# Rows of picks and of weights in the gating stage, built by one comparison and one product for each octet of tokens

## The chip, the cores and the metric

The kernel runs on one core of one Trainium2 chip. The metric is the device time of the core in microseconds (us); lower is better. The engines are TensorE (PE, with its weight loads as PEld), VectorE (DVE), ScalarE (ACT), GpSimd (POOL) and SyncE (SP), which issues most transfers.

## The reference, cut to what matters

Two layers over 256 latent and 256 context tokens of width 1024 are computed: a pooling mixer, then a gated DeltaNet mixer, each followed by a PEER expert mixer. The PEER mixer runs three times (context and latents in layer 0, latents in layer 1):

```python
sc, pos = lax.top_k(cand, PEER_TOPK)
...
eidx = jnp.take_along_axis(cidx, pos, axis=-1)   # 8 heads x 16 experts of 16384 for each token
gate = jax.nn.softmax(sc, axis=-1)
...
act = jax.nn.gelu(jnp.einsum('td,ted->te', xt, jnp.take(u_tab, et, axis=0)), approximate=False)
return jnp.einsum('te,ted->td', gt * act, jnp.take(v_tab, et, axis=0))
```

An expert is a pair (i1, i2) of keys, each of 0 to 127. So the weights of one token are a 128 x 128 matrix with up to 128 entries: the sum over its 128 picks of (one-hot row of i2) times (one-hot row of i1 scaled by the weight).

## The kernel before, in words

The kernel does not gather experts. It computes all 128 blocks of 128 experts for all tokens, multiplies the activations by the weight matrices, and multiplies the result with all of `v_tab`. Each of the three PEER passes (`peer(g, ...)`, g = 0, 1, 2) has these stages:

- **Query and U blocks.** Blocks of 512 KB are loaded to `raw[0..3]`; ScalarE rounds one to `hi` (line 542), VectorE takes the rest `lo` (line 1030), TensorE multiplies (lines 1732 to 1734), ScalarE applies Gelu into `buf` (line 577). VectorE finds the top picks beside it. Late in this stage `pick_pairs` turns the picks and the weights (split into three bf16 parts that sum to the fp32 weight) into bf16 arrays in which each value stands twice (`i1p`, `i2p`, `g_pairs`, by token), and computes the first rows of octets 0 and 1.
- **Gating stage.** 256 tokens are taken as 32 octets of 8 (`OCTET`, `N_OCT`). Even octets use the PSUM pair pG, odd ones pS; row buffers alternate in the same way. For octet o:
  - `first_row` (line 1152, VectorE): one comparison of 8 x 128 bf16 elements, column number against i1. It counts up `first_ready`.
  - `gate_hots` (VectorE): the same comparison against i2 (line 1158), then, after a wait on `first_ready`, three products (line 1162), one for each weight part, of 5 tokens x 128.
  - `gate_rows` or `gate_rows_at` (ScalarE, lines 592 and 600): the rows of the other 3 tokens (`ACT_GATED = 3`), 9 copies of 128 columns with the weight as scale, after a wait on `first_ready`.
  - `gate_octet` or `gate_matmuls` (TensorE, lines 1800 and 1787): 24 bf16 matmuls of 128 columns into one PSUM pair, after waits for VectorE's rows (`onehot`), ScalarE's rows (`rows_gated`) and the release of the PSUM pair by octet o - 2 (`gated`).
  - `apply_gates` (line 1174, VectorE): `buf` times PSUM, 1024 fp32 elements, after a wait on `gates_mm`.
- **V blocks.** As the U blocks, with TensorE lines 1863 to 1867.

VectorE's order in the gating stage is written out: the loop holds, for two octets, `apply_gates(o)`, then `onehot_rows(o + 2)`, which is `first_row` and `gate_hots`. In passes 0 and 1 TensorE also multiplies, behind the matmuls of each of the octets 0 to 27, one 512 KB chunk of the adaLN weights (`mod_chunk`, line 1813; the transfer is SP's line 487), and behind each odd octet from 5 on it turns a row into columns (`mod_columns`, line 1823), after ScalarE copied the row (`mod_row`, line 610). Pass 2 has neither.

At the end of the U blocks VectorE and ScalarE alternate between splitting the first V blocks and the rows of octets 0 and 1, since those rows lie in `raw`, where the last U blocks and the first V blocks were:

```python
for j in range(RING):
    split_lo(None, ku + NE - RING, j + AHEAD)
    if j == 1:
        ve.wait_ge(lo_ready, RING + k0 + NQ + NE)
        gate_hots(None, 0)
ve.wait_ge(lo_ready, RING + k0 + NQ + NE + AHEAD)
gate_hots(None, 1)
```

In loops an instruction whose address depends on the loop counter has a register instruction ahead of it ("ISA" or "REGISTER_ALU" in the order below, FUSED_REGOPS in the trace); where the instruction waits, the wait is on that register instruction.

Of the kernel before, what the change touches and what calls it, by code (L numbers as in the profile page):

```python
# [32 lines left out]
ALU = mybir.AluOpType  # L33
# [48 lines left out]
def build(nc, a, out):  # L82
    ctx = ExitStack()
    with ctx:
# [22 lines left out]
        table = sb("table", [P, 10])  # L107
        gated1 = sb("gated1", [P, 16, P])
        iota_b = sb("iota_b", [P, P], BF16)
# [212 lines left out]

        raw_flat = raw_all[:, :, :, :].rearrange("p r c e -> p (r c e)")
        hots = [halves(raw_flat[:, 2 * D:4 * D], 4, OCTET, P), halves(raw_flat[:, 0:2 * D], 4, OCTET, P)]
        gated_flat = gated1[:, :, :].rearrange("p a b -> p (a b)")
        first_rows = halves(gated_flat[:, 0:D], 2, OCTET, P)
        pairs = halves(gated_flat[:, D:2 * D], 4, T, 2)
        i1p, i2p = pairs[:, 0], pairs[:, 1]
        g_pairs = [pairs[:, 2], pairs[:, 3], halves(gT[:, :], T, 2)]
        bank_pair = [pG_pair, pS_pair]  # L330
# [177 lines left out]
        def _(act):  # L508
# [39 lines left out]
            def peer(g, k0, e0, last):  # L548
# [37 lines left out]
                def gate_rows(n, o):  # L586

                    act.wait_ge(first_ready, 2 * n + (N_OCT * g + o + 1) if n is not None else N_OCT * g + o + 1)
                    for t in range(OCTET - ACT_GATED, OCTET):
                        tok = 16 * n + (8 * o + t) if n is not None else 8 * o + t  # L590
                        for q in range(3):
                            i = s.activation(hots[o % 2][:, 1 + q, t, :], first_rows[:, o % 2, t, :], ACT.Copy, scale=picks[q][:, bass.ds(tok, 1)])  # L592
                    i.then_inc(rows_gated, 1)

                def gate_rows_at(n, o):

                    act.wait_ge(first_ready, OCTET * n + (N_OCT * g + o + 1))
                    for t in range(OCTET - ACT_GATED, OCTET):
                        for q in range(3):
                            i = s.activation(hots[o % 2][:, 1 + q, t, :], first_rows[:, o % 2, t, :], ACT.Copy,  # L600
                                             scale=picks[q][:, bass.ds(OCTET * OCTET * n + (OCTET * o + t), 1)])
                    i.then_inc(rows_gated, 1)
# [286 lines left out]
        def _(ve):  # L889
# [189 lines left out]
            def peer(g, k0, e0, last):  # L1079
# [32 lines left out]
                while b % RING:  # L1112
                    split_lo(None, ku + b, AHEAD)
                    b += 1
                assert b <= 88, b
                def pick_pairs(part):

                    if part == 0:
                        ve.wait_ge(picksT, g + 1)
                        v.tensor_copy(g_pairs[0], twice(pG[1][:, 0:T]))  # L1120
                        link(v.tensor_copy(i1p, twice(pG[0][:, 0:T])))
                    elif part == 1:
                        v.tensor_tensor(g_left, pG[1][:, 0:T], g_pairs[0][:, :, 0], ALU.subtract)
                        link(v.tensor_copy(i2p, twice(pG[0][:, T:2 * T])))
                    elif part == 2:
                        v.tensor_copy(g_pairs[1], twice(g_left))
                        link(v.tensor_copy(picks[0], g_pairs[0][:, :, 0]))
                    elif part == 3:
                        link(v.tensor_tensor(picks[2], g_left, g_pairs[1][:, :, 0], ALU.subtract))
                    elif part == 4:  # L1130
                        v.tensor_copy(g_pairs[2], twice(picks[2]))
                        link(v.tensor_copy(picks[1], g_pairs[1][:, :, 0]))
# [5 lines left out]
                twice = lambda x: x.unsqueeze(2).to_broadcast([P, T, 2])  # L1138

                def spread(x, m):  # L1140
                    return x.rearrange("p t (a b) -> p t a b", b=2)[:, 0:m]

                def per_token(x, tok, m):
                    return x[:, bass.ds(tok, m), :].unsqueeze(2).to_broadcast([P, m, P // 2, 2])

                def octet_cols():
                    return iota_b[:, :].rearrange("p (a b) -> p a b", b=2).unsqueeze(1).to_broadcast([P, OCTET, P // 2, 2])

                def first_row(n, o):

                    tok = 16 * n + 8 * o if n is not None else 8 * o
                    v.tensor_tensor(spread(first_rows[:, o % 2], OCTET), octet_cols(), per_token(i1p, tok, OCTET), ALU.is_equal).then_inc(first_ready, 1)  # L1152

                def gate_hots(n, o):

                    tok = 16 * n + 8 * o if n is not None else 8 * o
                    one, two = first_rows[:, o % 2], hots[o % 2]
                    v.tensor_tensor(spread(two[:, 0], OCTET), octet_cols(), per_token(i2p, tok, OCTET), ALU.is_equal)
                    ve.wait_ge(first_ready, 2 * n + (N_OCT * g + o + 1) if n is not None else N_OCT * g + o + 1)
                    m = OCTET - ACT_GATED  # L1160
                    for q in range(3):
                        i = v.tensor_tensor(spread(two[:, 1 + q], m), spread(one, m), per_token(g_pairs[q], tok, m), ALU.mult)  # L1162
                    i.then_inc(onehot, 1)

                def onehot_rows(n, o):

                    first_row(n, o)
                    gate_hots(n, o)

# [466 lines left out]
        def _(pe):  # L1636
# [111 lines left out]
            def peer(g, k0, e0, last):  # L1748
# [29 lines left out]
                def gate_matmuls(n, o):  # L1778
# [6 lines left out]
                    for t in range(OCTET):  # L1785
                        for q in range(3):
                            mm = t_.matmul(bank_pair[o % 2][:, t // QUAD, (t % QUAD) * P:(t % QUAD + 1) * P], hots[o % 2][:, 0, t, :],
                                           hots[o % 2][:, 1 + q, t, :], start=(q == 0), stop=(q == 2), skip_group_check=True)
                    mm.then_inc(gates_mm, 1)

                def gate_octet(n, o):
# [6 lines left out]
                    for t in range(OCTET):  # L1798
                        for q in range(3):
                            mm = t_.matmul(bank_pair[o % 2][:, t // QUAD, (t % QUAD) * P:(t % QUAD + 1) * P], hots[o % 2][:, 0, t, :],  # L1800
                                           hots[o % 2][:, 1 + q, t, :], start=(q == 0), stop=(q == 2), skip_group_check=True)
                    mm.then_inc(gates_mm, 1)
# [422 lines left out]
```

## Time and profile before

| | |
|---|---|
| median of 3 runs | 3440.96 us (3434.68 to 3442.36) |
| profiled execution | 3437.17 us, its span 3435.4 us |
| TensorE / VectorE / ScalarE busy | 94% / 65% / 48% of the span |
| mean granted TensorE clock | 0.964 of full speed |
| gating stages (first row product to last `apply_gates`) | 544 to 665 us, 1452 to 1573 us, 2944 to 3069 us |

A busy time is the sum of an engine's instruction durations, without overlap. In the timelines below, a start in us is followed by a duration in us; an instruction with no wait in front of it starts before the one ahead of it has ended, so its share of the engine's time is the distance from start to start, and not its duration. Brackets at the end of a line give the idle time before it and what ended that.

### The profile page before, as it was taken

Reading aid. Unit: us, or ns where it says so; the run is one execution under the profiler, and the core shown is the slowest. Engines: PE = TensorE matmul, PEld = TensorE weight load, DVE = VectorE, ACT = ScalarE, POOL = GpSimd, SP = SyncE. Lnnn points to the kernel's source line nnn. Section 1 sums busy time; section 2 is a strip of 40 time slices with the busy share of each in tenths; the row PEclk is TensorE's granted clock in tenths of the full one; section 3 lists DMA queues with packets and bytes.
Section 4 is the critical chain, followed back from the end, with each engine's and each line's share of the span. In section 5 each row is a group of like instructions: output and inputs, shape, how many; then the busy total and the mean of one; then the engine's idle time right before and its main releaser. Section 6 shows DMA issues by size and latency. Waiting matters only on the chain.

```text
span 3435.4 us, 73133 instructions
## 1 busy us (share of the span) xinstructions
PE 3239.5 (94%) x25548; PEld 2864.7 (83%) x25548; DVE 2223.0 (65%) x4624; ACT 1665.2 (48%) x2924; POOL 152.6 (4%) x90
## 2 busy tenths in 40 slices
PE   8999999999999999999999998889889999669998
PEld 4899996588889999957888898877789999658887
DVE  6588957855556887596555673443348884785555
ACT  5544446645444444575545553222234444664544
POOL 0000000000000000000000362011100000000000
PEclk9999999999999999999999998998899999879999
DMA  8555454355565555454656441000145545116664
GB/s 320 172 166 182 165 188 161 129 195 191 196 208 165 182 182 172 161 166 151 216 193 206 151 146 57 3 2 2 44 153 177 183 165 183 48 68 194 204 193 135
DMA packets 143454, 530.33 MB, mean 154 GB/s; under 512 B 16544, under 2 KB 16688, under 8 KB 141040
## 3 DMA queue, kind: packets, MB, share of 16 engines
q1 hardware_dynamic: 141120, 514.01, 45.2%
q0 software_dynamic: 2224, 14.76, 1.2%
q8 instruction: 80, 1.31, 0.2%
q14 instruction: 30, 0.25, 0.0%
HBM read 522.42 MB, written 6.29 MB: 154 GB/s over the span
## 4 chain that ended last, share of the span: by engine, by line
PE 76%; DVE 12%; issue 7%; POOL 2%; ACT 1%; DVEq 1%; DMA 1%; SPq 0%; ACTq 0%; POOLq 0%
PE pS L1732 11%; PE pS L1734 11%; PE pS L1733 11%; PE pY L1863 10%; PE pY L1865 10%; PE pY L1867 10%; PE pY L1925 4%; PE pS L1925 3%; DVE buf L1174 2%; POOL lo L1608 2%; PE pG L1925 2%; DVE raw L1162 2%; DVE gated L1152 1%; DVE lo L1030 1%; DVE buf L1264 1%
## 5 line engine op out<-in xcount | busy, mean ns | idle before, releaser
L1030 DVE TENSOR_TENSOR lo<-raw,hi 128x1024 fp32r<-128x1024 f32 x824 | 1009.4, 1225 | 774.7 <-ACT hi L542 771.5
L542 ACT CAST hi<-raw 128x1024 fp32r<-128x1024 f32 x872 | 913.3, 1048 | 526.3 <-PE pY L1867 510.0
L1732 PE MATMUL pS<-h_hi,hi 128*128 128x256 f32 x3552 | 1013.0, 285 | 32.9 <-DVE lo L1030 9.9
L1733 PE MATMUL pS<-h_lo,hi 128*128 128x256 f32 x3552 | 1007.6, 284 | 0.0
L1734 PE MATMUL pS<-h_hi,lo 128*128 128x256 f32 x3552 | 1007.3, 284 | 0.0
L1732 PEld LDWEIGHTS pS<-h_hi,hi 128*128 128x128 f32 x3552 | 684.2, 193 | 40.3 <-issue 27.6
L1733 PEld LDWEIGHTS pS<-h_lo,hi 128*128 128x128 f32 x3552 | 684.5, 193 | 0.2
L1734 PEld LDWEIGHTS pS<-h_hi,lo 128*128 128x128 f32 x3552 | 684.3, 193 | 0.0
L1863 PE MATMUL pY<-hi,h_hi 128*128 128x512 f32 x1536 | 475.4, 391 | 7.0 <-DVE h_lo L1215 7.0
L1867 PE MATMUL pY<-hi,h_lo 128*128 128x512 f32 x1536 | 474.7, 390 | 0.0
L1865 PE MATMUL pY<-lo,h_hi 128*128 128x512 f32 x1536 | 474.7, 390 | 0.0
L577 ACT ACTIVATE buf<-pS 128x256 f32 x372 | 142.8, 384 | 602.9 <-PE pS L1734 602.9
L1863 PEld LDWEIGHTS pY<-hi,h_hi 128*128 128x128 f32 x1536 | 289.6, 189 | 67.6 <-issue 6.6
L1865 PEld LDWEIGHTS pY<-lo,h_hi 128*128 128x128 f32 x1536 | 289.6, 189 | 60.3
L1867 PEld LDWEIGHTS pY<-hi,h_lo 128*128 128x128 f32 x1536 | 289.5, 188 | 60.4
L592 ACT ACTIVATE raw<-gated,g 128x128 bf16<-128x128 bf16 x576 | 175.2, 388 | 52.9 <-DVE gated L1152 51.9
L1215 DVE TENSOR_TENSOR h_lo<-buf,h_hi 128x256 fp32r<-128x256 f32 x384 | 160.6, 418 | 2.4 <-ACT h_hi L648 2.4
L648 ACT CAST h_hi<-buf 128x256 fp32r x384 | 154.6, 403 | 11.8 <-DVE buf L1174 11.8
L1608 POOL TENSOR_TENSOR lo<-raw,hi 128x1024 fp32r<-128x1024 f32 x48 | 116.1, 2431 | 186.8 <-ACT hi L542 186.6
L1925 PE MATMUL pY<-buf 64*64 64x64 f32 (+2 forms) x2956 | 107.2, 228 | 13.6 <-DVE buf L1451 9.9
L1925 PEld LDWEIGHTS pY<-buf 64*64 64x64 f32 (+2 forms) x2956 | 100.4, 144 | 19.5 <-DVE buf L1451 10.5
L1732 PE MATMUL pY<-h_hi,hi 128*128 128x256 f32 x352 | 103.2, 293 | 8.6 <-POOL lo L1608 5.0
(298 smaller groups left out, 3261.3 us busy)
## 6 DMA issues: line engine op xcount, KB each, us to landing
raw<-in_blocks SPq DMA_DIRECT2D x872, 512.0 KB, 3.3
gate_mod<-in_mod_wT SPq DMA_DIRECT2D x56, 512.0 KB, 3.6
raw<-in_mod_wT SPq DMA_DIRECT2D x20, 512.0 KB, 9.4
buf<-in_mod_wT SPq DMA_DIRECT2D x20, 512.0 KB, 8.2
buf<-in_keysT POOLq DMA_DIRECT2D x3, 1024.0 KB, 5.5
buf<-in_window SPq DMA_DIRECT2D x2, 1024.0 KB, 11.7
spill_x_res<-buf POOLq DMA_DIRECT2D x2, 1024.0 KB, 4.8
spill_x_h<-buf POOLq DMA_DIRECT2D x2, 1024.0 KB, 7.2
```

The lines of the kernel that those rows point to most:

```text
L542: s.copy(hi[slot][:, :, :], raw[slot][:, :, :]).then_inc(hi_ready, 1)
L592: i = s.activation(hots[o % 2][:, 1 + q, t, :], first_rows[:, o % 2, t, :], ACT.Copy, scale=picks[q][:, bass.ds(tok, 1)])
L1030: v.tensor_tensor(lo[slot][:, :, :], raw[slot][:, :, :], hi[slot][:, :, :].bitcast(F32), ALU.subtract).then_inc(lo_ready, 1)
L1215: v.tensor_tensor(h_lo[:, j:j + 1, :], buf[:, bass.ds(b, 1), :] if n is not None else buf[:, b:b + 1, :], h_hi[:, j:j + 1, :].bitcast(F32) ...
L1608: g_.tensor_tensor(lo[slot][:, :, :], raw[slot][:, :, :], hi[slot][:, :, :].bitcast(F32), ALU.subtract).then_inc(lo_ready, 1)
L1732: t_.matmul(out, hi[slot][:, c, :], h_hi[:, c, :], start=(c == 0), stop=False)
L1733: t_.matmul(out, hi[slot][:, c, :], h_lo[:, c, :], start=False, stop=False)
L1734: mm = t_.matmul(out, lo[slot][:, c, :], h_hi[:, c, :], start=False, stop=(c == NC - 1))
L1863: t_.matmul(pY[:, 2 * r + s_, :], w1, rows_of(hi[slot], s_), start=first, stop=False, skip_group_check=True)
L1865: t_.matmul(pY[:, 2 * r + s_, :], w1, rows_of(lo[slot], s_), start=False, stop=False, skip_group_check=True)
L1867: mm = t_.matmul(pY[:, 2 * r + s_, :], w2, rows_of(hi[slot], s_), start=False, stop=lastb, skip_group_check=True)
L1925: return t_.matmul(o, l, x, start=start, stop=stop, skip_group_check=True)
```

## The change: rows and picks by octet

The two comparisons of an octet become one of 2 x 1024 elements, and the three products become one of 1920 elements. For this, picks lie by octet, i1 beside i2 (`picks_p`), and weights by octet, the three parts beside each other (`gates_p`). The first rows move from `gated1` into `raw`, ahead of the gated rows; `raw` and `gated1` become one tensor, so that both destinations of the comparison are reached with one stride. Octets 0 and 1 no longer get their first rows in `pick_pairs`. The comparison counts up `first_ready` at its end, and the product behind it waits on that count. The number and size of ScalarE's and TensorE's instructions, and of the transfers, stay the same.

```diff
-        raw_all = sb("raw", [P, RING, NC, P])
+        weights_rows = sb("raw", [P, RING * D + 2 * D])
+        raw_all = weights_rows[:, 0:RING * D].rearrange("p (r c e) -> p r c e", r=RING, c=NC)
...
+        N_DVE = OCTET - ACT_GATED
+        raw_rows = halves(weights_rows[:, 0:RING * D], 2, 4 * OCTET, P)
+        second_rows = halves(weights_rows[:, RING * D:(RING + 1) * D], 2, OCTET, P)
+        first_rows = raw_rows[:, :, 0:OCTET]
+        all_rows = halves(weights_rows[:, 0:(RING + 1) * D], 10, OCTET, P)
+        both_rows = [all_rows[:, 0:9:8], all_rows[:, 4:10:5]]
+        gated_rows = [raw_rows[:, :, OCTET:OCTET + 3 * N_DVE], raw_rows[:, :, OCTET + 3 * N_DVE:]]
...
                     if part == 0:
                         ve.wait_ge(picksT, g + 1)
-                        v.tensor_copy(g_pairs[0], twice(pG[1][:, 0:T]))
-                        link(v.tensor_copy(i1p, twice(pG[0][:, 0:T])))
+                        v.tensor_copy(part_b, pG[1][:, 0:T])
+                        link(v.tensor_copy(picks_p[:, :, 0], octets(pG[0][:, 0:T])))
...
                     elif part == 5:
+                        gate_part(1)
+                        gate_part(2)
                         v.memset(mark[:, 4:5], 0.0).then_inc(parts_ready, 1)
-                    else:
-                        first_row(None, part - 6)
...
-                def first_row(n, o):
-
-                    tok = 16 * n + 8 * o if n is not None else 8 * o
-                    v.tensor_tensor(spread(first_rows[:, o % 2], OCTET), octet_cols(), per_token(i1p, tok, OCTET), ALU.is_equal).then_inc(first_ready, 1)
-
-                def gate_hots(n, o):
-
-                    tok = 16 * n + 8 * o if n is not None else 8 * o
-                    one, two = first_rows[:, o % 2], hots[o % 2]
-                    v.tensor_tensor(spread(two[:, 0], OCTET), octet_cols(), per_token(i2p, tok, OCTET), ALU.is_equal)
...
+                def rows_of_picks(n, o):
+
+                    cols = iota_b[:, :].rearrange("p (a b) -> p a b", b=2).unsqueeze(1).to_broadcast([P, 2 * OCTET, P // 2, 2])
+                    tok = picks_p[:, bass.ds(octet_of(n, o), 1)].rearrange("p o k t b -> p (o k t) b")
+                    v.tensor_tensor(both_rows[1 - o % 2].rearrange("p k t e -> p k (t e)"), cols,
+                                    tok.unsqueeze(2).to_broadcast([P, 2 * OCTET, P // 2, 2]), ALU.is_equal).then_inc(first_ready, 1)
+
+                def rows_of_gates(n, o):
+
                     ve.wait_ge(first_ready, 2 * n + (N_OCT * g + o + 1) if n is not None else N_OCT * g + o + 1)
-                    m = OCTET - ACT_GATED
-                    for q in range(3):
-                        i = v.tensor_tensor(spread(two[:, 1 + q], m), spread(one, m), per_token(g_pairs[q], tok, m), ALU.mult)
-                    i.then_inc(onehot, 1)
+                    rows = gated_rows[0][:, 1 - o % 2].rearrange("p t (a b) -> p t a b", b=2)
+                    tok = gates_p[:, bass.ds(octet_of(n, o), 1)].rearrange("p o q t b -> p (o q t) b")
+                    first = first_rows[:, 1 - o % 2, 0:N_DVE]
+                    v.tensor_tensor(rows, first.rearrange("p t e -> p (t e)").unsqueeze(1).to_broadcast([P, 3, N_DVE * P]),
+                                    tok.unsqueeze(2).to_broadcast([P, 3 * N_DVE, P // 2, 2]), ALU.mult).then_inc(onehot, 1)
...
                     if j == 1:
                         ve.wait_ge(lo_ready, RING + k0 + NQ + NE)
-                        gate_hots(None, 0)
+                        onehot_rows(None, 0)
                 ve.wait_ge(lo_ready, RING + k0 + NQ + NE + AHEAD)
-                gate_hots(None, 1)
+                onehot_rows(None, 1)
```

What VectorE executes for one octet in the loop of the gating stage, before (1174 is `apply_gates`, 1152 and 1158 the comparisons, 1162 the products; `gated` is the old home of the first rows):

```order
L1174 TENSOR_TENSOR buf<-buf,pG 128x128x8
L1152 ISA
L1152 TENSOR_TENSOR gated<-iota_b,gated 128x1024
L1158 ISA
L1158 TENSOR_TENSOR raw<-iota_b,gated 128x1024
L1159 REGISTER_ALU
L1162 ISA [waits first_ready]
L1162 TENSOR_TENSOR raw<-gated 128x640
L1162 ISA
L1162 TENSOR_TENSOR raw<-gated 128x640
L1162 ISA
L1162 TENSOR_TENSOR raw<-gated,gT 128x640
```

The wait on `first_ready` has the second comparison between itself and the instruction that it waits for.

The same place in the changed kernel (1183 is `apply_gates`, 1162 the comparison, 1171 the product):

```order
L1183 ISA [waits gates_mm]
L1183 TENSOR_TENSOR buf<-buf,pG 128x128x8
L1162 ISA
L1162 TENSOR_TENSOR raw<-iota_b,raw 128x2x1024
L1167 REGISTER_ALU
L1171 ISA [waits first_ready]
L1171 TENSOR_TENSOR raw<-raw 128x1920
```

The wait, with its register instruction, now stands right behind the instruction that it waits for.

VectorE ahead of the loop, in the changed kernel (1042 is `split_lo`, 1204 the loop's start):

```order
L1042 TENSOR_TENSOR lo<-raw,hi 128x1024 [waits hi_ready] x2
L1162 TENSOR_TENSOR raw<-iota_b,raw 128x2x1024 [waits lo_ready]
L1171 TENSOR_TENSOR raw<-raw 128x1920 [waits first_ready]
L1042 TENSOR_TENSOR lo<-raw,hi 128x1024 [waits hi_ready] x2
L1162 TENSOR_TENSOR raw<-iota_b,raw 128x2x1024 [waits lo_ready]
L1171 TENSOR_TENSOR raw<-raw 128x1920 [waits first_ready]
L1204 UNCONDITIONAL_BRANCH [waits evacuated]
```

The comparisons against i1 of octets 0 and 1 stood many U blocks earlier before; now they stand here, behind the last splits.

## Rows read from the trace of the kernel before

**Rows 1.** Windows: start:end, length, busy us, granted clock, DMA; first and third gating stage

```profile
553.00:657.00 104.00, 99.87 (x860) 52.83 (x860) 103.09 (x176) 82.81 (x276) 0.00 (x0) 1.00 0.43 139
2955.00:3062.00 107.00, 60.10 (x681) 53.77 (x678) 102.04 (x173) 78.63 (x260) 0.00 (x0) 0.73 0.00 0
```

**Rows 2.** Timeline of VectorE, one octet in the first gating stage

```profile
571.68 1.23 DVE L1174 TENSOR_TENSOR buf<-buf,pS 128x1024 f32 x1
572.81 0.70 DVE L1152 TENSOR_TENSOR gated<-iota_b,gated 128x1024 bf16<-128x1024 bf16 x1
573.41 0.70 DVE L1158 TENSOR_TENSOR raw<-iota_b,gated 128x1024 bf16<-128x1024 bf16 x1
574.01 0.90 DVE L1162 TENSOR_TENSOR raw<-gated 128x640 bf16<-128x640 bf16 x2
...
575.22 1.23 DVE L1174 TENSOR_TENSOR buf<-buf,pG 128x1024 f32 x1
```

**Rows 3.** Timeline of TensorE, two octets in the first gating stage

```profile
576.61 1.51 PE L1800 MATMUL pS<-raw 128*128 128x128 bf16 x24
578.06 1.88 PE L1813 MATMUL pY<-gate_mod,small 128*2 128x512 f32 x4
579.87 0.60 PE L1823 MATMUL pY<-ident,g 2*128 2x2 f32 x4
580.40 1.51 PE L1800 MATMUL pG<-raw 128*128 128x128 bf16 x24
```

**Rows 4.** Timeline of the third gating stage, one round of the pS octets, three engines

```profile
2979.14 1.22 DVE L1174 TENSOR_TENSOR buf<-buf,pS 128x1024 f32 x1 [0.62 <-PE pS L1787]
2980.28 0.69 DVE L1152 TENSOR_TENSOR gated<-iota_b,gated 128x1024 bf16<-128x1024 bf16 x1
...
2981.10 2.73 ACT L592 ACTIVATE raw<-gated,g 128x128 bf16<-128x128 bf16 x9 [1.50 <-DVE gated L1152]
...
2984.07 2.74 PE L1787 MATMUL pS<-raw 128*128 128x128 bf16 x24 [1.49 <-DVE buf L1174]
...
2986.95 1.22 DVE L1174 TENSOR_TENSOR buf<-buf,pS 128x1024 f32 x1 [0.60 <-PE pS L1787]
```

**Rows 5.** Timeline of TensorE, third gating stage: first and last of the slow octets, last octet

```profile
2968.45 2.74 PE L1787 MATMUL pS<-raw 128*128 128x128 bf16 x24 [2.00 <-DVE buf L1174]
...
3055.02 2.74 PE L1787 MATMUL pG<-raw 128*128 128x128 bf16 x24 [0.84 <-ACT raw L592]
...
3066.41 1.51 PE L1787 MATMUL pS<-raw 128*128 128x128 bf16 x24 [2.05 <-DVE buf L1174]
```

**Rows 6.** Timeline of VectorE, late in the first U stage: an awaited instruction, then one not awaited

```profile
417.97 2.28 DVE L1261 TENSOR_TENSOR buf<-buf,iota 128x2048 f32<-128x2048 f32 x1
420.29 1.23 DVE L1030 TENSOR_TENSOR lo<-raw,hi 128x1024 fp32r<-128x1024 f32 x1
421.43 2.29 DVE L1264 TENSOR_TENSOR buf<-buf 128x2048 f32<-128x2048 f32 x1
```

**Rows 7.** Timeline of VectorE, ScalarE and TensorE at the start of the third gating stage

```profile
2944.36 0.69 DVE L1158 TENSOR_TENSOR raw<-iota_b,gated 128x1024 bf16<-128x1024 bf16 x1
...
2952.90 1.22 DVE L1174 TENSOR_TENSOR buf<-buf,pG 128x1024 f32 x1
...
2956.44 1.22 DVE L1174 TENSOR_TENSOR buf<-buf,pS 128x1024 f32 x1
...
2944.91 2.73 ACT L592 ACTIVATE raw<-gated,g 128x128 bf16<-128x128 bf16 x9
...
2951.09 2.74 ACT L592 ACTIVATE raw<-gated,g 128x128 bf16<-128x128 bf16 x9 [0.32 <-DVE lo L1030]
...
2953.97 1.50 PE L1800 MATMUL pS<-raw 128*128 128x128 bf16 x24 [2.27 <-ACT raw L592]
```

**Rows 8.** Timeline of VectorE, the last `apply_gates` of the first gating stage

```profile
664.14 1.22 DVE L1174 TENSOR_TENSOR buf<-buf,pS 128x1024 f32<-128x1024 f32 x1 [2.69 <-PE pS L1800]
```

**Rows 9.** The page's costliest groups: the splits; busy, mean ns, idle before

```profile
L1030 DVE TENSOR_TENSOR lo<-raw,hi 128x1024 fp32r<-128x1024 f32 x824 | 1009.4, 1225 | 774.7 <-ACT hi L542 771.5
```

More of the change, by code:

```diff
@@ L1115, in peer, with gate_part @@
                 assert b <= 88, b
+                octets = lambda x: x.rearrange("p (o t) -> p o t", t=OCTET).unsqueeze(3).to_broadcast([P, N_OCT, OCTET, 2])
+                def gate_part(q):
+                    v.tensor_copy(gates_p[:, :, q], octets(picks[q])[:, :, 0:N_DVE])
                 def pick_pairs(part):
@@ L1119, in pick_pairs @@
                         ve.wait_ge(picksT, g + 1)
-                        v.tensor_copy(g_pairs[0], twice(pG[1][:, 0:T]))
-                        link(v.tensor_copy(i1p, twice(pG[0][:, 0:T])))
+                        v.tensor_copy(part_b, pG[1][:, 0:T])
+                        link(v.tensor_copy(picks_p[:, :, 0], octets(pG[0][:, 0:T])))
                     elif part == 1:
-                        v.tensor_tensor(g_left, pG[1][:, 0:T], g_pairs[0][:, :, 0], ALU.subtract)
-                        link(v.tensor_copy(i2p, twice(pG[0][:, T:2 * T])))
+                        v.tensor_copy(picks_p[:, :, 1], octets(pG[0][:, T:2 * T]))
@@ L1125, in pick_pairs @@
+                        link(v.tensor_copy(picks[0], part_b))
                     elif part == 2:
-                        v.tensor_copy(g_pairs[1], twice(g_left))
-                        link(v.tensor_copy(picks[0], g_pairs[0][:, :, 0]))
+                        link(v.tensor_tensor(g_left, pG[1][:, 0:T], picks[0], ALU.subtract))
+                        gate_part(0)
                     elif part == 3:
-                        link(v.tensor_tensor(picks[2], g_left, g_pairs[1][:, :, 0], ALU.subtract))
+                        link(v.tensor_copy(part_b, g_left))
@@ L1130, in pick_pairs @@
                     elif part == 4:
-                        v.tensor_copy(g_pairs[2], twice(picks[2]))
-                        link(v.tensor_copy(picks[1], g_pairs[1][:, :, 0]))
+                        link(v.tensor_copy(picks[1], part_b))
+                        link(v.tensor_tensor(picks[2], g_left, picks[1], ALU.subtract))
                     elif part == 5:
+                        gate_part(1)
+                        gate_part(2)
                         v.memset(mark[:, 4:5], 0.0).then_inc(parts_ready, 1)
-                    else:
-                        first_row(None, part - 6)
@@ L1154, in gate_hots, with octet_of @@
-                def gate_hots(n, o):
-                    tok = 16 * n + 8 * o if n is not None else 8 * o
-                    one, two = first_rows[:, o % 2], hots[o % 2]
-                    v.tensor_tensor(spread(two[:, 0], OCTET), octet_cols(), per_token(i2p, tok, OCTET), ALU.is_equal)
-                    ve.wait_ge(first_ready, 2 * n + (N_OCT * g + o + 1) if n is not None else N_OCT * g + o + 1)
-                    m = OCTET - ACT_GATED
-                    for q in range(3):
-                        i = v.tensor_tensor(spread(two[:, 1 + q], m), spread(one, m), per_token(g_pairs[q], tok, m), ALU.mult)
-                    i.then_inc(onehot, 1)
+                def octet_of(n, o):
+                    return 2 * n + o if n is not None else o
@@ L1165, in onehot_rows @@
                 def onehot_rows(n, o):
-                    first_row(n, o)
-                    gate_hots(n, o)
+                    rows_of_picks(n, o)
+                    rows_of_gates(n, o)
                 def apply_gates(n, o):
@@ L1799, in gate_octet @@
                         for q in range(3):
-                            mm = t_.matmul(bank_pair[o % 2][:, t // QUAD, (t % QUAD) * P:(t % QUAD + 1) * P], hots[o % 2][:, 0, t, :],
-                                           hots[o % 2][:, 1 + q, t, :], start=(q == 0), stop=(q == 2), skip_group_check=True)
+                            mm = t_.matmul(bank_pair[o % 2][:, t // QUAD, (t % QUAD) * P:(t % QUAD + 1) * P], second_rows[:, 1 - o % 2, t, :],
+                                           gated_row(o, t, q), start=(q == 0), stop=(q == 2), skip_group_check=True)
                     mm.then_inc(gates_mm, 1)
```

32 lines of the change are left out of this document (13 added, 19 removed).

## The prediction

> **What bounds the kernel now.** I read the windows first. TensorE is busy for nearly the whole span outside the gating stages, and the change touches it nowhere else, so only these three stages count. In the first (the second reads the same) VectorE is busy 103.09 of 104 us and TensorE 99.87, at a clock of 1.00; in the third VectorE is busy 102.04 of 107 us, TensorE 60.10, at a mean clock of 0.73 [rows 1]. So I need three limits for an octet.
>
> - VectorE's own time. From start to start in [rows 2]: `apply_gates` 1.13 us, each comparison 0.60, the three products 575.22 - 574.01 = 1.21, so 0.40 each. Sum 3.54.
> - TensorE's own time in the first two stages: 24 matmuls 1.45, chunk 1.81, columns 0.53 in every second octet [rows 3]. Two octets: 2 x 3.26 + 0.53 = 7.05 against VectorE's 7.08. Both are at their limit.
> - The chain through the engines. Octet o + 2 needs in turn: `apply_gates(o)`, first rows, ScalarE's nine copies, matmuls, `apply_gates(o + 2)`. [Rows 4] show one round at the half clock (1.2 GHz): 1.14 to the comparison, 0.69 + 0.13 to ScalarE, 2.97 to TensorE, 2.88 to the next `apply_gates`: 7.81 for two octets. That is above 7.08, and VectorE waits 0.6 in each round. At 2.4 GHz the matmuls take 1.51 in place of 2.74 [rows 5, 4], so the round is 6.58, which VectorE's 7.08 hides with 0.5 us to spare.
>
> In the third stage the clock goes back and forth: 14 of the 32 octets ran at 1.2 GHz; the first and last of them are in [rows 5].
>
> **The change, part by part.** VectorE instructions, from two sizes in [rows 2]: 1024 bf16 elements in 0.60 us and 640 in 0.40 give 0.52 ns an element and 0.07 us fixed. The comparison of 2048 then takes 1.13 to the next start (0.07 less than two), and ends after 1.22, as the 1024 fp32 elements of `apply_gates` do. The product of 1920 takes 1.07 (0.13 less than three). With nothing else, an octet would cost 3.34 instead of 3.54.
>
> Two things are given back. First, the wait on `first_ready`. Before, the second comparison stood between; now VectorE waits for the end of the instruction just ahead of it. [Rows 6] show such a wait without a register instruction: 417.97 + 2.28 = 420.25, next start 420.29, where an instruction not awaited is followed by the next one 0.09 before its end (420.29 + 1.23 against 421.43). That is 0.13 lost, the low bound. In the loop the wait is on a register instruction; the nearest row is ScalarE's, which in the loop starts 0.13 behind the end of the comparison [rows 4]. So the product starts 1.22 + 0.14 = 1.36 after the comparison, the high bound, which I take because it has the same form. VectorE's octet: 1.13 + 1.36 + 1.07 = 3.56, or 3.46 by the low bound, against 3.54: nothing is gained, or 0.08.
>
> Second, ScalarE waits for the comparison of both rows: 1.22 instead of 0.69. The chain grows by 0.53 a round, to 7.11 at 2.4 GHz and 8.34 at 1.2 GHz. At 2.4 GHz even the low bound for VectorE (6.92) no longer hides it. So **the round goes from 7.08 to about 7.12 at 2.4 GHz and from 7.81 to 8.34 at 1.2 GHz**.
>
> The Trainium skill, VectorE: DVE Perf Modes, section on the TRN2 errata, says that the Vector engine pays a fixed cost once per instruction, 58 cycles, and the section "The DRAIN you can't avoid" that a semaphore costs nothing extra. By these two the octet would cost about 3.36 (an estimate from that page), and the sum would be some 17 us faster. The first agrees with the 0.07 us of the row; the second does not agree with the 0.13 us of the awaited instruction here, and neither speaks of ScalarE's later start.
>
> First and second stage, each:
> - Start: the first rows of octets 0 and 1 are now made between the last splits. In the first stage TensorE waits there for a transfer anyway, which hides most. Walking the engines through it gives +0.3.
> - 28 octets at 0.02 to 0.04 more: +0.8.
> - TensorE: octet o + 1's matmuls come 3.79 behind octet o's where columns stand between [rows 3], while VectorE comes round in 3.56. When the chain has no spare, this delays the next `apply_gates` by about 0.16, once in four octets in the looped part: +0.7.
> - End: the last two octets hang on the chain alone (VectorE waits 2.69 before the last `apply_gates` [rows 8]): +0.5.
>
> Together 2.3, twice: 4.6.
>
> Third stage:
> - Start [rows 7]: ScalarE's rows of octet 0 wait for a comparison now begun at 2944.36 and start at 2945.61 instead of 2944.91, and everything behind them (split, split) 0.7 later. ScalarE's rows of octet 1 now start at 2951.80 + 1.22 + 0.03 = 2953.05 instead of 2951.09; TensorE's matmuls of octet 1 at 2955.93; VectorE, at `apply_gates(0)` by 2954.15 instead of 2952.90, is free for `apply_gates(1)` at 2957.74 instead of 2956.44. +1.3.
> - Seven slow rounds: 7 x 0.53 = +3.7. 14 fast octets: +0.4. End, as above: +0.5.
>
> Together 5.9. The rest: `pick_pairs` does other copies, in VectorE's pauses between splits, of which it has 0.94 us for each split on average (774.7 us over 824 [rows 9]); uncovered, its few extra copies of some 0.3 us would cost 1 us a stage at most. I cost it at nothing. ScalarE's, TensorE's and SP's instructions stay.
>
> Sum: 4.6 + 5.9 = **+10.5 us**. On the profiled execution's 3437.17 that is 3447.7. It lies 3.8 below the median of the three runs, on which the same sum gives 3451.5. I take 3450.
>
> **Rivals.**
> - *The smaller count pays.* If ScalarE's start and the wait did not matter, 94 octets would save 0.20 each: 19 us less, 3422. For it: VectorE is the busiest engine of all three stages [rows 1]. Against it: the round of 7.81 in [rows 4] is the chain's, so the chain exists, and it had only 0.5 to spare. It would need the comparison to release ScalarE by 0.7 us. The skill's rules above give this case. 4%.
> - *The clock of the third stage stays high.* The seven rounds above 7.08 cost 5.1 us before. If the shifted rhythm kept 2.4 GHz, they would go: 4.6 + 1.3 + 0.8 + 0.5 - 5.1 = +2, 3443. For it: the clock came and went in this stage under one and the same rhythm, so its pattern hangs on small shifts. Against it: TensorE does the same work in a longer round. 14%.
> - *The clock stays low there.* 15 rounds at 8.34 make 125.1 against 7 x 7.81 + 8 x 7.08 = 111.3: 13.8 + 1.8 + 4.6 = +20, 3461. For it: the low clock's rounds have longer pauses now. 7%.
> - *The new address patterns halve the rate.* The destination has two pieces and the product repeats an input. At the rate of `apply_gates` (1024 elements in 1.13) both instructions would take 2 us more: some +190 us. Against it: each innermost run is still two adjacent bf16 values, as before. 2%.
>
> **How the numbers follow.** The forecast (chains as worked out) has 73%. Within 0.2% is 6.9 us, about what a measurement of this kernel can tell from no change; the three runs themselves span 7.7. From the forecast's +10.5 with some 4 us either way (the wait by its low bound, the share of slow octets, the runs' spread) about one part in five falls within 0.2%. Slower: 0.73 x 0.8 and the two slow rivals, 0.67. Faster: 0.04 and a small rest, 0.06. The same: 0.27. The range 3440 to 3460 takes in the high-clock rival and nearly reaches the low-clock one; beyond it lie about 2 in 10.
>
> **What the changed profile would show.** VectorE's comparison of 2 x 1024 lasts 1.22 and the product starts 1.36 behind it (1.26: the low bound). ScalarE starts 1.35 behind the comparison's start. Rounds of two octets: 7.1 to 7.3 in the first two stages, 8.34 where the third runs at 1.2 GHz. VectorE's busy time in the gating stages falls by some 0.1 us an octet while idle time before the product and before `apply_gates` rises by more. TensorE's idle time there, before matmuls, ends with ScalarE. The second `apply_gates` of the third stage comes 1.3 later. I am wrong if ScalarE starts at 0.8 behind the comparison, if `apply_gates` never waits at 2.4 GHz and comes every 3.4 us, or if the third stage has far fewer or more than 14 slow octets.

## The result: 0.4% slower

| | before | changed |
|---|---|---|
| median of 6 runs each | 3436.65 us | 3452.69 us |
| lowest and highest | 3434.68, 3442.36 | 3448.75, 3456.99 |
| ratio, 95% interval | | 1.0043 (1.0031 to 1.0056) |
| span of the profiled execution | 3435.4 us | 3450.0 us |

The forecast was 10.5 us more (3450, range 3440 to 3460). The medians differ by 16.0, the profiled spans by 14.7. A later measurement of the same kernel against other runs of the kernel before gave 1.0035 (1.0023 to 1.0048).

The page of the changed kernel: VectorE has 282 fewer instructions and 10.7 us less busy time than before (2223.0 us), and the kernel is slower.

```profile
span 3450.0 us, 72563 instructions
...
PE 3241.9 (94%) x25548; PEld 2866.6 (83%) x25548; DVE 2212.3 (64%) x4342; ACT 1665.4 (48%) x2924; POOL 152.6 (4%) x90
```

The windows that answer to [rows 1], first stage and third (the third starts 5 us later and is 10 us longer):

```profile
553.00:657.00 104.00, 98.70 (x839) 51.47 (x840) 99.48 (x88) 82.67 (x274) 0.00 (x0) 1.00 0.44 139
2960.00:3077.00 117.00, 62.37 (x720) 55.88 (x717) 101.72 (x89) 81.28 (x268) 0.00 (x0) 0.73 0.00 0
```

VectorE is busy 99.5 of 104 us instead of 103.1: it now stands still in the first stage too. The timeline of one octet there, to lay beside [rows 2] (1183 is `apply_gates`, 1162 the comparison, 1171 the product):

```profile
568.70 1.21 DVE L1183 TENSOR_TENSOR buf<-buf,pG 128x1024 f32 x1
569.84 1.22 DVE L1162 TENSOR_TENSOR raw<-iota_b,raw 128x2048 bf16<-128x2048 bf16 x1
571.21 1.16 DVE L1171 TENSOR_TENSOR raw<-raw 128x1920 bf16<-128x1920 bf16 x1 [0.15 <-DVE raw L1162]
572.28 1.22 DVE L1183 TENSOR_TENSOR buf<-buf,pS 128x1024 f32 x1
```

From start to start: 1.14, 1.37, 1.07, so 3.58 instead of 3.54. The comparison lasts 1.22; then comes an idle time of 0.15, ended by VectorE's own comparison. Three instructions fewer are worth 0.20, and the wait costs 0.24.

The third stage at 1.2 GHz, three engines, one round of the pG octets, beside [rows 4]:

```profile
2981.74 1.22 DVE L1183 TENSOR_TENSOR buf<-buf,pG 128x1024 f32 x1 [1.11 <-PE pG L1796]
2982.88 1.22 DVE L1162 TENSOR_TENSOR raw<-iota_b,raw 128x2048 bf16<-128x2048 bf16 x1
...
2984.24 2.74 ACT L604 ACTIVATE raw<-raw,g 128x128 bf16<-128x128 bf16 x9 [2.05 <-DVE raw L1162]
...
2987.22 2.74 PE L1796 MATMUL pG<-raw 128*128 128x128 bf16 x24 [2.05 <-ACT raw L604]
...
2990.11 1.22 DVE L1183 TENSOR_TENSOR buf<-buf,pG 128x1024 f32 x1 [1.12 <-PE pG L1796]
```

ScalarE starts 1.36 behind the comparison's start (before 0.82), TensorE 2.98 behind ScalarE, the next `apply_gates` 2.89 behind TensorE. The round is 8.37 where it was 7.81, and VectorE waits 1.1 in it instead of 0.6. Over the whole third stage, who ended VectorE's idle time before `apply_gates`, before and then changed:

```profile
  PE pS L1787: 6.7, 9
```

```profile
  PE pG L1796: 9.8, 9
  PE pS L1796: 2.4, 1
  PE pS L1809: 1.1, 1
```

6.7 us in 9 waits became 13.3 in 11; in each kernel one of them, the last `apply_gates` of the stage, is the longest (1.75 and 2.43). The third line of the changed kernel is at the stage's start, which answers to [rows 7]:

```profile
2955.55 1.23 DVE L1162 TENSOR_TENSOR raw<-iota_b,raw 128x2048 bf16<-128x2048 bf16 x1
...
2957.88 1.21 DVE L1183 TENSOR_TENSOR buf<-buf,pG 128x1024 f32 x1
...
2962.62 1.22 DVE L1183 TENSOR_TENSOR buf<-buf,pS 128x1024 f32 x1 [1.08 <-PE pS L1809]
...
2956.87 2.74 ACT L604 ACTIVATE raw<-raw,g 128x128 bf16<-128x128 bf16 x9 [2.34 <-DVE raw L1162]
...
2959.75 2.72 PE L1809 MATMUL pS<-raw 128*128 128x128 bf16 x24 [4.36 <-ACT raw L604]
```

TensorE pauses 4.36 us for ScalarE's rows of octet 1 (before 2.27), and runs that octet at 1.2 GHz, where it ran at 2.4 GHz before.

**Where the 14.7 us lie.** I cut both timelines at the start of the last U matmul and the start of the first V matmul of each pass.

| stretch | before | changed | more |
|---|---|---|---|
| first gating stage | 116.9 | 118.0 | +1.1 |
| V blocks to the next gating stage | 790.7 | 789.7 | -1.0 |
| second gating stage | 116.7 | 117.7 | +1.0 |
| V blocks, DeltaNet, to the third | 1375.6 | 1378.1 | +2.5 |
| third gating stage | 120.5 | 129.7 | +9.2 |
| V blocks and end | 364.8 | 366.6 | +1.8 |

The first line starts 0.1 later. The last goes with the clock: the first V blocks of this pass had 5.7 us at 1.2 GHz, before none. Windows of them, before and then changed (the clock is the third figure from the end):

```profile
3068.00:3080.00 12.00, 8.76 (x38) 6.98 (x39) 7.75 (x10) 5.76 (x10) 0.00 (x0) 1.00 0.82 290
```

```profile
3081.00:3093.00 12.00, 9.51 (x30) 7.62 (x31) 6.21 (x8) 5.51 (x9) 0.00 (x0) 0.66 0.77 271
```

### The profile page after: what moved, and what is told of

Same layout as the page of the kernel before. It is cut to its first block, busy times and chain, and to the rows that moved or that the text cites. A ratio compares the mean times of both kernels' runs of the same rounds, so it can differ in the third digit from the quotient of the medians.

```text
span 3450.0 us, 72563 instructions
## 1 busy us (share of the span) xinstructions
PE 3241.9 (94%) x25548; PEld 2866.6 (83%) x25548; DVE 2212.3 (64%) x4342; ACT 1665.4 (48%) x2924; POOL 152.6 (4%) x90
## 4 chain that ended last, share of the span: by engine, by line
PE 81%; DVE 8%; issue 6%; ACT 3%; POOL 2%; DMA 0%; ACTq 0%; DVEq 0%; SPq 0%; POOLq 0%
PE pS L1741 11%; PE pS L1743 11%; PE pS L1742 11%; PE pY L1872 10%; PE pY L1876 10%; PE pY L1874 10%; PE pY L1934 4%; PE pS L1934 3%; PE pY L1822 2%; POOL lo L1617 2%; PE pG L1934 2%; PE pS L1809 1%; ACT raw L604 1%; DVE raw L1162 1%; DVE lo L1042 1%
## 5 line engine op out<-in xcount | busy, mean ns | idle before, releaser
L604 ACT ACTIVATE raw<-raw,g 128x128 bf16<-128x128 bf16 x576 | 175.2, 388 | 65.2 <-DVE raw L1162 65.2
L1171 DVE TENSOR_TENSOR raw<-raw 128x1920 bf16<-128x1920 bf16 x96 | 111.2, 1158 | 14.1 <-DVE raw L1162 13.9
L1162 DVE TENSOR_TENSOR raw<-iota_b,raw 128x2048 bf16<-128x2048 bf16 x96 | 117.0, 1219 | 0.2
```

What stands on the lines that cost most here:

```text
L604: i = s.activation(gated_row(o, t, q), first_rows[:, 1 - o % 2, t, :], ACT.Copy, scale=picks[q][:, bass.ds(tok, 1)])
```

## The experiments

My theory: **the chain** from `apply_gates` through the comparison, ScalarE and TensorE sets the rounds, because ScalarE is released late; at 2.4 GHz it is about as long as VectorE's own time, at 1.2 GHz much longer. Rivals: VectorE's own sum with the new wait; the moved tensors; a slow product. All kernels below were also timed against the kernel before, in three series on three chips, each with its own runs of the kernel before; so kernels of different series are compared by their ratios. This table has their gating stages, cut as above, and the octets of the third stage at 1.2 GHz; both come from one profile of each kernel.

| kernel | 1st | 2nd | 3rd | octets at 1.2 GHz | ratio to before, interval |
|---|---|---|---|---|---|
| before | 116.9 | 116.7 | 120.5 | 14 | |
| changed | 118.0 | 117.7 | 129.7 | 15 | 1.0043 (1.0031 to 1.0056) |
| changed, again | 118.0 | 117.7 | 129.8 | 15 | 1.0035 (1.0023 to 1.0048) |
| layout alone | 116.9 | 115.4 | 119.5 | 10 | 1.0006 (0.9997 to 1.0015) |
| two comparisons, one product | 114.7 | 114.2 | 113.4 | 3 | 0.9970 (0.9959 to 0.9981) |
| one comparison, three products | 121.9 | 121.7 | 132.0 | 18 | 1.0066 (1.0052 to 1.0081) |
| early first rows | 112.0 | 112.1 | 110.3 | 2 | 0.9952 (0.9938 to 0.9966) |
| warm, before | 117.0 | 115.5 | 114.6 | 0 | 0.9980 (0.9971 to 0.9989) |
| warm, changed | 118.0 | 118.9 | 118.8 | 1 | 1.0002 (0.9992 to 1.0012) |
| early first rows, three products | 114.2 | 114.2 | 114.4 | 18 | 0.9970 (0.9958 to 0.9981) |
| one product, with a memset | 114.6 | 114.3 | 113.8 | 2 | 0.9970 (0.9957 to 0.9983) |
| one product, octets spaced | 114.5 | 114.4 | 120.4 | 10 | 0.9988 (0.9979 to 0.9996) |
| early first rows, early start | 112.1 | 112.1 | 109.4 | 0 | 0.9936 (0.9924 to 0.9949) |

### The layout alone

```diff
-        raw_all = sb("raw", [P, RING, NC, P])
+        weights_rows = sb("raw", [P, RING * D + 2 * D])
+        raw_all = weights_rows[:, 0:RING * D].rearrange("p (r c e) -> p r c e", r=RING, c=NC)
...
-        gated1 = sb("gated1", [P, 16, P])
+        gated1 = weights_rows[:, RING * D:RING * D + 2 * D].rearrange("p (a b) -> p a b", a=16)
```

> The kernel before, with raw and gated1 as one tensor (the addresses of the changed kernel) and nothing else changed. In the changed kernel's profile 3.7 us of the growth lie between the second and the third gating stage, where no instruction was changed. Chain theory (only the gating stages matter, the rest is where the granted clock happened to fall): within 3 us of the kernel before, the octets of the gating stages as before (3.54 us apart at 2.4 GHz). Layout theory (the moved tensors cost time): 3 to 5 us slower, all of it between the stages.

1.0006, no difference that can be told; but the interval reaches 5 us, so the time alone doesn't rule out the 3 to 5 us of the layout theory. The stretch between the second and third gating stage does: it took 1376.8 us, 1.2 more than in the kernel before (1375.6), and in the changed kernel's second profile, with the same layout, 1374.7. The layout falls. (By the cut of the table above, the changed kernel's growth there is 2.5 us, not the 3.7 of the expectation.) The octets of the gating stages come in the same order and 3.54 apart as before, and yet 10 of the third stage ran at 1.2 GHz instead of 14: the clock's pattern differs between profiles of nearly the same code.

### Two comparisons, one product

```diff
-                    v.tensor_tensor(both_rows[1 - o % 2].rearrange("p k t e -> p k (t e)"), cols,
-                                    tok.unsqueeze(2).to_broadcast([P, 2 * OCTET, P // 2, 2]), ALU.is_equal).then_inc(first_ready, 1)
+                    row_of_pick(n, o, 0).then_inc(first_ready, 1)
+                    row_of_pick(n, o, 1)
```

> The changed kernel with its comparison split again into two (first rows, then second rows; ScalarE is released by the first), the product of 1920 kept. Chain theory: ScalarE starts 0.8 behind the comparison again, the chain is 6.6 a round at 2.4 GHz and 7.8 at 1.2 GHz, VectorE's octet 1.13 + 0.60 + 0.60 + 1.07 = 3.40; so the third stage's rounds fall to 6.8 at 2.4 GHz, those of the first two stay at TensorE's 7.05, and the whole is 1 to 5 us faster than the kernel before. Rival (one product of 1920 or the layout is what costs): 5 us or more slower than before, with a product longer than 1.16.

3427.19 us against 3437.9 us: 10.7 faster, twice the best that I expected. So one product of 1920 is a gain, and the one comparison, with the wait behind it, is what costs. VectorE's octet in the third stage, from its timeline (two comparisons in the line of x2):

```profile
2976.14 1.21 DVE L1188 TENSOR_TENSOR buf<-buf,pG 128x1024 f32 x1
2977.27 1.28 DVE L1163 TENSOR_TENSOR raw<-iota_b,raw 128x1024 bf16<-128x1024 bf16 x2
2978.48 1.15 DVE L1176 TENSOR_TENSOR raw<-raw 128x1920 bf16<-128x1920 bf16 x1
2979.55 1.21 DVE L1188 TENSOR_TENSOR buf<-buf,pS 128x1024 f32 x1
```

3.41 (3.40 was reckoned), with no idle time: `first_ready` was counted up one comparison earlier. What I had not reckoned with is the clock. Windows of the third stage, 0.95 of full speed against 0.73 in [rows 1]:

```profile
2960.00:3062.00 102.00, 47.62 (x709) 42.27 (x707) 98.53 (x115) 78.62 (x259) 0.00 (x0) 0.95 0.00 0
```

After octets 2 to 4 at 1.2 GHz, TensorE kept 2.4 GHz for the 27 behind them.

### One comparison, three products

```diff
...
+                    first = first_rows[:, 1 - o % 2, 0:N_DVE].rearrange("p t (a b) -> p t a b", b=2)
+                    for q in range(3):
+                        rows = gated_rows[0][:, 1 - o % 2, N_DVE * q:N_DVE * (q + 1)].rearrange("p t (a b) -> p t a b", b=2)
+                        tok = gates_p[:, bass.ds(octet_of(n, o), 1), q].rearrange("p o t b -> p (o t) b")
+                        i = v.tensor_tensor(rows, first, tok.unsqueeze(2).to_broadcast([P, N_DVE, P // 2, 2]), ALU.mult)
+                    i.then_inc(onehot, 1)
```

> The changed kernel with its product split again into three, the comparison of 2048 kept. Chain and wait theory together: VectorE's octet 1.13 + 1.37 + 1.21 = 3.71, so rounds of 7.4 at 2.4 GHz in all stages and 8.36 at 1.2 GHz; 20 to 27 us slower than the kernel before. Rival (only ScalarE's later start costs, VectorE's own sum is never the limit): rounds as in the changed kernel (7.16), and 14 to 18 us slower than before.

3460.9 against 3437.9, 23 slower, in the range of the theory. Where the octets of its third stage are slow, the rounds took about 8.36, as expected. The octets of the first stage, from VectorE's timeline, are 3.73 apart (wait included), so with a wait of this kind VectorE's own sum is a limit as well:

```profile
578.68 1.22 DVE L1184 TENSOR_TENSOR buf<-buf,pG 128x1024 f32 x1
579.82 1.22 DVE L1162 TENSOR_TENSOR raw<-iota_b,raw 128x2048 bf16<-128x2048 bf16 x1
581.19 1.29 DVE L1172 TENSOR_TENSOR raw<-raw 128x640 bf16<-128x640 bf16 x3 [0.16 <-DVE raw L1162]
582.41 1.21 DVE L1184 TENSOR_TENSOR buf<-buf,pS 128x1024 f32 x1
```

### Early first rows

If the chain is the limit, taking `apply_gates` and the comparison out of it must help more than any shorter instruction.

```diff
+                def first_row(n, o):
+                    ve.wait_ge(rows_gated, 2 * n + (N_OCT * g + o - 1))
+                    row_of_pick(n, o, 0).then_inc(first_ready, 1)
...
-                        apply_gates(n, o)
-                        onehot_rows(n, o + 2)
+                        first_row(n, o + 2)
+                        apply_gates(n, o)
+                        other_rows(n, o + 2)
...
+                    if n is not None or o >= 2:
+                        act.wait_ge(gates_mm, 2 * n + (N_OCT * g + o - 1) if n is not None else N_OCT * g + o - 1)
```

> As the run with two comparisons and one product, but VectorE makes the first rows of octet o + 2 ahead of apply_gates(o), after a wait for ScalarE's rows of octet o, and ScalarE's copies for o + 2 wait for the matmuls of octet o. So neither apply_gates nor a comparison stands in the chain. Chain theory: the chain is then matmuls, copies, matmuls, about 4.8 a round at 2.4 GHz and 6.1 at 1.2 GHz, under VectorE's 6.8: VectorE never waits in the third stage at either clock, which takes about 109 us instead of 115, and the kernel is 6 to 12 us faster than before. Rival (the clock alone slows the third stage, by whatever path): rounds above 7.5 at 1.2 GHz again, and a gain of 3 us at most over the run with two comparisons.

3421.86 against 3437.9: 16 faster, again more than expected (6 to 12). But only 2 octets of its third stage ran at 1.2 GHz, so it says little about rounds at that clock. The gain over the kernel with two comparisons comes from all three stages (112.0, 112.1, 110.3 against 114.7, 114.2, 113.4).

### A third stage with the clock kept up

```diff
                     mm.then_inc(gates_mm, 1)
+                    for w in range(20):
+                        t_.matmul(pY[:, 0, 0:P], iota_b[:, :], iota_b[:, :], start=True, stop=True, skip_group_check=True)
```

> The kernel before with 20 extra bf16 matmuls of constants into an unused PSUM bank behind each octet from 2 on of the third gating stage, to keep TensorE busy in its pauses; in passes 0 and 1 nothing differs. If they keep the clock at 2.4 GHz, the rounds are 7.08 throughout (a chain of 6.6 is hidden), the eight waits of 0.62 go, and the kernel is 3 to 6 us faster than before. If the clock falls all the same, TensorE's own 24 + 20 matmuls at 1.2 GHz (4.7 us an octet) become the limit and it is 15 us or more slower.

> The changed kernel with the same 20 extra matmuls. Chain theory with the clock as an amplifier: at a steady 2.4 GHz its third stage has rounds of 7.16, so it is only 3 to 6 us slower than the warm kernel before (start 1.3, 30 octets at 0.04, end 0.5, and 1 to 2 in the first two stages). Rival (the later start of ScalarE costs what it costs at any clock, the clock's changes are incidental): it stays 12 us or more slower than the warm kernel before.

The clock stayed up, but for octet 1 of the changed kernel; windows of the third stage, first the warm kernel before, then the warm changed one:

```profile
2955.00:3062.00 107.00, 76.78 (x1288) 71.74 (x1286) 107.00 (x183) 82.66 (x273) 0.00 (x0) 1.00 0.00 0
```

```profile
2960.00:3071.00 111.00, 78.79 (x1300) 73.79 (x1300) 105.27 (x93) 84.05 (x277) 0.00 (x0) 0.98 0.00 0
```

Adding matmuls made the kernel before faster: 3432.53 against 3440.42. The warm changed kernel takes 3440.41, so the change costs 7.9 us there. That is above the 3 to 6 of the theory and well below the 12 of the rival. In the third stage alone the difference is 118.8 - 114.6 = 4.2 instead of 9.2: 2.5 up to the second `apply_gates`, 1.3 in the octets up to the last but one, which are 3.58 apart instead of 3.54, and 0.4 at the end. So **4 of the 9 us are there with the clock kept up, and 5 come only with the low clock**, at which the longer chain sets the rounds. Each of these figures rests on one profile of each kernel. What lies above 6 is in the second stage (3.4), where both kernels run the code without extra matmuls and the clock fell at another moment; I leave it open how much of that would stay over many profiles.

### Early first rows with three products

> The kernel with early first rows, but with three products again, so VectorE's octet is 3.54 as in the kernel before. The clock of the third stage should then fall now and then as before, which it did not in the kernels whose octets are 3.41 apart. Chain theory: apply_gates never waits for TensorE even in the octets at 1.2 GHz, the third stage's 30 octets are all 3.54 apart, and the kernel is 3 to 6 us faster than before. Rival (the gain of the early rows came only through the clock that stayed high): waits of 0.6 in slow octets, and within 2 us of the kernel before.

This run decides on the rounds at 1.2 GHz. The edit takes the product apart as above, in the kernel with early first rows. 18 octets ran at 1.2 GHz, and after the first, 2.74 us matmuls come 3.54 apart. TensorE and VectorE, from their timelines:

```profile
2959.34 2.74 PE L1814 MATMUL pG<-raw 128*128 128x128 bf16 x24 [1.20 <-ACT raw L606]
2962.78 2.74 PE L1814 MATMUL pS<-raw 128*128 128x128 bf16 x24 [0.70 <-ACT raw L606]
```

```profile
2959.51 1.22 DVE L1200 TENSOR_TENSOR buf<-buf,pS 128x1024 f32 x1
...
2963.05 1.22 DVE L1200 TENSOR_TENSOR buf<-buf,pG 128x1024 f32 x1
...
2966.59 1.23 DVE L1200 TENSOR_TENSOR buf<-buf,pS 128x1024 f32 x1
```

```profile
2955.00:3062.00 107.00, 67.48 (x721) 60.75 (x722) 107.00 (x183) 83.49 (x276) 0.00 (x0) 0.70 0.00 0
```

VectorE is busy 107.00 of 107 at a mean clock of 0.70, lower than in the kernel before. With the same instructions as there and another order, `apply_gates` does not wait for slow matmuls: in this stage its only idle time above 0.1 us is the one before the last. The rounds of 7.8 were the chain's. The kernel is 10 us faster than before (3430.36 against 3440.42); I had expected 3 to 6, and had left out the ends of the first two stages, where the last octets hang on the chain (114.2 against 116.9 and 116.7).

### Is it the spacing that keeps the clock up?

```diff
+                    if g == 2:
+                        v.memset(g_left[:, 0:64], 0.0)
```

> The kernel with two comparisons and one product, plus a memset of 64 columns for each octet of the third stage, so that the octets there are about 3.54 apart again instead of 3.41. If the clock stays at 2.4 GHz because of the spacing of 3.41, it now falls again in about half of the octets, the waits of 0.6 return, and the kernel is 8 to 11 us slower than the one without the memset, near the kernel before. If the spacing has nothing to do with it, it is slower by 30 times 0.13, 4 us, and the clock stays high.

The memset took next to no time: `apply_gates` follows 0.02 behind its start, and the octets stayed 3.42 apart. The ratio is 0.9970, as without it; the question was not tested. The second try put a product of 128 bf16 elements in its place:

> The kernel with two comparisons and one product again, now plus a product of 128 bf16 elements for each octet of the third stage (by the fit of the two sizes, 0.13 us), since the memset of the last try added only 0.01. The octets of that stage should be 3.54 apart instead of 3.41. If the clock stays at 2.4 GHz because of the spacing of 3.41, it now falls again in about half of the octets, and the kernel is 7 to 11 us slower than the one without the addition. If the spacing has nothing to do with it, the clock stays high and it is 4 us slower.

```profile
2981.22 1.22 DVE L1190 TENSOR_TENSOR buf<-buf,pG 128x1024 f32 x1
...
2984.76 1.21 DVE L1190 TENSOR_TENSOR buf<-buf,pS 128x1024 f32 x1
```

Now the octets are 3.54 apart at 2.4 GHz, and the clock fell in 10 of 32, mean 0.82:

```profile
2955.00:3062.00 107.00, 55.02 (x696) 49.14 (x696) 103.69 (x147) 79.99 (x264) 0.00 (x0) 0.82 0.00 0
```

The median is 3435.79, 8.6 above the kernel without the addition; by the two ratios, which are what compares across series, it is 6.2, between the two answers expected. The third stage takes 7.0 more, of which 30 x 0.13 = 4 are VectorE's; the rest comes with the slow octets. So a spacing of 3.41 or 3.42 went with 0 to 3 slow octets (four kernels) and 3.54 or more with 10 to 18 (all others but the two with extra matmuls). What in the chip makes that so, these runs don't tell, and each count is from one profile.

### The start, and the changed kernel once more

```diff
+        first_rows = halves(weights_rows[:, RING * D:(RING + 1) * D], 2, OCTET, P)
+        second_rows = raw_rows[:, :, 0:OCTET]
...
+                    elif part >= 6:
+                        row_of_pick(None, part - 6, 0).then_inc(first_ready, 1)
```

> The kernel with early first rows, with the homes of first and second rows exchanged, so that the first rows of octets 0 and 1 are made during the U blocks again, as in the kernel before. Theory of the start: in all kernels that make them behind the last splits, the second apply_gates of the third stage comes 7.1 us or more behind the last U matmul, before it was 6.4; 1 us or a little more returns in the third stage and less in the first two, 16 to 20 us faster than the kernel before. Rival (the start is hidden by other waits): no difference from the kernel with early rows.

3416.83 us, and 0.9936 (22 us faster, above the 16 to 20 expected) where the kernel with early rows had 0.9952: the intervals meet, so the gain from the start is likely and not sure. The third stage is 0.9 shorter, the first two are the same; its second `apply_gates` comes 6.7 behind the last U matmul instead of 7.6, which is that 0.9. VectorE's octet in this kernel, the best of all (1168 are the comparisons, the second of them already for the octet after):

```profile
2948.88 1.22 DVE L1201 TENSOR_TENSOR buf<-buf,pG 128x1024 f32 x1
2950.01 0.68 DVE L1168 TENSOR_TENSOR raw<-iota_b,raw 128x1024 bf16<-128x1024 bf16 x1
2950.61 1.15 DVE L1181 TENSOR_TENSOR raw<-raw 128x1920 bf16<-128x1920 bf16 x1
2951.68 0.68 DVE L1168 TENSOR_TENSOR raw<-iota_b,raw 128x1024 bf16<-128x1024 bf16 x1
2952.29 1.21 DVE L1201 TENSOR_TENSOR buf<-buf,pS 128x1024 f32 x1
```

> The changed kernel itself once more, beside the same runs of the kernel before as the others. In its profile 2.5 us of the growth lie between the second and the third gating stage, and in the warm kernel, which is the same up to there, that stretch is 0.2 us longer than in the kernel before. Theory (the stretch only varies with the clock): it comes out between 1375 and 1382 us again and not always above the kernel before's 1375.6; 12 to 17 us slower than before in all. Rival (part of the growth is there): 2 us or more over the kernel before there once more, though the layout alone showed 1.2.

The stretch between the second and third gating stages took 1374.7 us, less than in the kernel before. So the 2.5 us there are not shown to be the change's. The third gating stage took 129.8 again, with 15 octets at 1.2 GHz, and the V blocks and the end 366.5 again.

## Why the prediction was right, and where its terms were off

- **What was luck.** 3450 lies 2.7 below the measured 3452.69, but it was set between two bases. On the median of six runs of the kernel before, 3436.65, the forecast's sum gives 3447.2, which is 5.5 short. And where the profiles differ by 14.7, the three gating stages make 11.3, for the 10.5 forecast, only because two misses offset each other: 2.1 instead of 4.6 in the first two, 9.2 instead of 5.9 in the third. The other 3.4 lie outside these stages, where nothing was forecast; 1.8 of them are the V blocks at 1.2 GHz.
- **The comparison** of 2048 lasts 1.22, **the product** 1.07 to the next start, as fitted from two sizes. **The wait** costs its high bound: 1.37 where 1.36 was taken. The low bound did not hold in the loop.
- **ScalarE's later start**, 0.53 a round forecast: the rounds at 1.2 GHz went to 8.37 (forecast 8.34). The run with two comparisons takes this part back, and the run with early rows and three products shows the same chain by removing it.
- **First and second stage**: forecast 2.3 each, measured 1.1 and 1.0. The start came as walked (0.3 and 0.2 more at the second `apply_gates`). The 28 octets from the third `apply_gates` to the last but one took 1.5 more (100.6 against 99.1), as much as the 0.8 and 0.7 forecast, but split otherwise: VectorE's own octet grew by 0.04, which makes 1.1, and TensorE delayed `apply_gates` by 0.17, as forecast, but in two octets only. (Once in four octets would have been about 1, not 0.7.) The term that failed is the end, -0.8 where +0.5 was forecast: the clock fell later, no octet ran at 1.2 GHz there (before, one did), and the last two octets became shorter, not longer.
- **Third stage**: forecast 5.9, measured 9.2. Start: 2.5 for 1.3. TensorE began octet 1 2.1 later, about as walked (2.0), but behind its pause of 4.36 this octet ran at 1.2 GHz, 1.2 us longer. In the other two kernels with a pause of 4.36 or 4.37 there it was slow as well; where the pause was 3.3 or less it was not, or only in part. Octets: 6.1 for 4.1. End: 0.7 for 0.5. I gave each slow round 0.53 more. But the clock came and went more often (at 1.2 GHz were octet 1, then four groups of three, then the last two; before, three groups of four or five), and every group of three slow octets holds two waits of 1.1. So nearly the same number of slow octets (15 for 14) holds more waits: 9 of 1.1 where the forecast had seven long rounds. After the stage, 1.8 more for V blocks at 1.2 GHz, not forecast.
- **The rival that the smaller count pays** (4%) fell as stated; the fixed cost of an instruction is real, and the kernel with two comparisons collects the product's part of it. The Trainium skill's sentence in VectorE: DVE Perf Modes, "The DRAIN you can't avoid", that a semaphore costs nothing extra (measured there on a row of copies), does not hold here for a wait on the instruction just ahead in a loop: 0.15 idle, 0.24 more from start to start.
- **The clock rivals** (14% and 7%): neither came, with 15 slow octets for 14. The kernels above had from 0 to 18, so the forecast of an unchanged count was in part luck. The low clock made 5 of the 9 us of the third stage.

## What to carry to other kernels

Before two instructions of an engine are fused, ask who waits for the first of them: here 0.20 us of fixed costs were saved an octet, another engine's start was moved back by 0.53, and a wait was laid bare that cost VectorE 0.24. A chain through several engines is shortened by order, not by instruction count: making the small input of the next round ahead of the long instruction took 10 us off the kernel before with the same instructions, and 16 together with the fused product; the fused comparison with the fused product put 12 to 16 on it (the two measurements). And where TensorE pauses between bursts, test the change at both clocks.

## What I had not expected of the hardware

- With octets 3.41 us apart TensorE ran all but 0 to 3 of the third stage's 32 octets at 2.4 GHz; with octets 3.54 apart it ran 10 to 18 of them at 1.2 GHz, though its work was the same. 20 useless matmuls behind each octet from 2 on of this stage made the kernel before 0.2% faster.
- A 64-column memset between two VectorE instructions with no wait cost 0.01 us, a product of 128 bf16 elements 0.13.
- The stretch from the second gating stage's end to the third's start took 1374.7 to 1381.4 us in kernels that run nearly the same code there. A single profile can't tell 2 us there.
